# The recurrent stage of an RWKV-7 block: masks, squares and scaling by ScalarE, blocks picked by rows of 32, and one decay of the state

## The chip, the cores and the metric

The kernel runs on one core of a Trainium2 chip. The core has TensorE (PE), VectorE (DVE), ScalarE (ACT), GpSimd (POOL) and SyncE (SP), which here issues all transfers. The time is in device microseconds for the whole program, three transformer-like blocks over 2048 positions of width 1024. It is compared as the median over executions.

## The reference

The part that matters is the recurrence of the second block. It has 8 heads of 64 channels, and a 64 by 64 state per head that is decayed and changed at every position:

```python
def step(state, inp):
    rt, wt, kt, vt, kkt, at = inp
    sa = jnp.einsum('bhvk,bhk->bhv', state, -kkt)
    state = (state * wt[:, :, None, :]
             + sa[..., :, None] * (kkt * at)[..., None, :]
             + vt[..., :, None] * kt[..., None, :])
    yt = jnp.einsum('bhvk,bhk->bhv', state, rt)
    return state, yt

mean = jnp.mean(y, axis=-1, keepdims=True)
var = jnp.mean(jnp.square(y - mean), axis=-1, keepdims=True)
y = ((y - mean) * lax.rsqrt(var + GN_EPS)).reshape(B, S, D_RWKV)
y = y * gn_g.astype(jnp.float32) + gn_b.astype(jnp.float32)
bonus = jnp.sum((r_h * k_h * r_k).astype(jnp.float32), axis=-1, keepdims=True) * v_h.astype(jnp.float32)
y = y + bonus.reshape(B, S, D_RWKV)
```

The result is then multiplied by the silu of a gate. All of it is float32.

## The kernel before

The program is a row of stages, each with its own tiles (a prefix such as `rw_`) and semaphores. Every stage walks over 16 tiles of 128 positions. `rwkv` is the stage of the recurrence; an earlier one (`rwkv_project`) has stored r, kk, b, k, v and the gate, already multiplied by the decays inside a tile, in `packed`, and the decays across a tile in `totals` (`e_tot`, two factors per tile: to its middle, and from its middle to its end).

Within a tile the recurrence is a triangular system of 128 unknowns per head. Step i of the pipeline prepares tile i and, on the same engines, finishes tile t = i - 1. Each engine runs its own list in the order in which it is written, and waits on counting semaphores:

- TensorE multiplies b by kk and r (`multiply(i, pi, 0, r)`, L1569), which gives the products BA in banks 0 to 3, and later k by kk and r (banks 6, 7, 4, 5), which gives KA. In between it forms Z (`solve`, L1623 and L1626), four matmuls whose result nobody reads (the fillers, L1666), the rows of the 16 by 16 diagonal blocks spread over all partitions (`spread`, L1577 and L1578), the solution SA = XT Z, the output Y and the change of the state (`read_out`, L1636 to L1650).
- VectorE masks the products for the diagonal blocks and adds them up to a compact form (`compact_blocks`), masks BA, inverts all blocks of 16 together in 15 steps of two instructions (`invert_blocks`; tiles `outer` and `Ys`), writes the inverse into XT, renews the state S, and masks KA.
- The inverse then grows from blocks of 16 to 32, 64 and 128 in three levels (l = 4, 5, 6). At each, TensorE multiplies X by the corner of BA that joins two blocks (stage 0, L1600), ScalarE copies the product to T1 (L1730), TensorE multiplies by the inverse (stage 1, L1610 for X and L1613 for XT), and VectorE subtracts the result from X and XT. The corner is CT, which GpSimd makes as BA times a mask (L1748), two instructions of four heads per level.
- After levels 4 and 5, TensorE turns the inputs of tile i + 1 (`turn_two`, L1555) and ScalarE copies them (L1703 krT, L1705 bT and kT).
- The group norm of tile t runs on VectorE between the levels (`finish`: the mean, y less the mean, the squares and their sum), GpSimd takes the power -0.5, and in the next step `put_out` multiplies by gain and rstd and adds `rest`. GpSimd makes gain and rest (L1754 to L1766).

The state S is decayed twice in a tile, each time as a 128 by 512 product on VectorE (L1788): at the start of a step to the middle of the tile, and in `renew_state` to its end. Level 4's stage 1 waits for `inc_taken`, since it writes the bank from which the state's change is read. In the loop over tiles two steps stand in one iteration; the first three and the last two steps are written out.

## Time and profile before

| | |
|---|---|
| median of 3 runs | 4566.32 us (4563.86 to 4570.67) |
| the profiled execution | 4565.9 us, span 4563.8 us |
| mean granted TensorE clock | 0.963 |
| TensorE busy in the whole span | 4174.7 us (91%) |
| VectorE, ScalarE, GpSimd busy in the span | 2632.5, 1344.7, 633.4 us |
| the recurrent stage, first to last instruction | about 1702 to 2354 us |

The timeline lists an engine's instructions in order, with equal neighbours merged. "Idle before" in square brackets names what the profile holds for the releaser. Starts and durations of matmuls overlap, since they are pipelined, so the distance between two starts is the measure of pace. A group of 16 matmul records stands for 8 float32 matmuls.

### The profile page before, as it was taken

To read this page: it belongs to the slowest core of one execution; us is meant where nothing else is said; L and a number is where in the kernel's file an instruction comes from. 1 tells how busy PE (TensorE), PEld (TensorE's weight loads), DVE (VectorE), ACT (ScalarE), POOL (GpSimd) and SP (SyncE) were. 2 spreads that over 40 slices of the span, in tenths; PEclk is the share of its full clock that TensorE was granted. 3 is DMA by queue.
4 is the path that set the end of the run, shared out by engine and by line. 5 is a ranking of instruction groups with operands and counts; after the bars stand their busy time and mean duration, and the time that the engine had idled before them with its cause. 6 is when DMAs were issued, how large, how long until landed. Compare 5 with 4: busy or idle time off the path is not lost. (4 is left out here: it accounts for less than half of the span.)

```text
span 4563.8 us, 68323 instructions
## 1 busy us (share of the span) xinstructions
PE 4174.7 (91%) x24935; PEld 3522.7 (77%) x24992; DVE 2632.5 (58%) x5109; ACT 1344.7 (29%) x2721; POOL 633.4 (14%) x585
## 2 busy tenths in 40 slices
PE   9999799999799978999979996999989899899889
PEld 7888678887577758899978885778778677677667
DVE  5444444444566766888863345788743443677743
ACT  4323322222322221222221114666621211323221
POOL 0000011122000002333321110000000111122200
PEclk9999899999899988999989997999999999999989
DMA  3111311111444431111132325210034323423333
GB/s 147 49 64 64 130 62 63 62 62 55 168 135 140 140 123 53 50 48 48 49 115 110 115 101 172 77 35 20 10 139 164 129 103 135 135 90 98 99 132 115
DMA packets 218707, 434.13 MB, mean 95 GB/s; under 512 B 36819, under 2 KB 90836, under 8 KB 218422
## 3 DMA queue, kind: packets, MB, share of 16 engines
q1 hardware_dynamic: 218550, 432.09, 27.7%
q8 instruction: 93, 1.52, 0.1%
q14 instruction: 64, 0.52, 0.0%
HBM read 248.40 MB, written 146.93 MB: 87 GB/s over the span
## 5 line engine op out<-in xcount | busy, mean ns | idle before, releaser
L265 PE MATMUL rp_pj<-rp_w_high,rp_hT_high 128*128 128x512 f32 (+1 forms) x640 | 236.3, 378 | 22.7 <-DVE rp_gate L1429 17.8
L2569 DVE TENSOR_SCALAR_CACHE_REDUCE fa_sm<-fa_sc 128x512 f32<-128x512 f32 (+2 forms) x320 | 194.5, 610 | 92.6 <-PE fa_sc L2410 81.9
L265 PE MATMUL fp_pj<-fp_w_high,fp_hT_high 128*128 128x512 f32 (+2 forms) x640 | 216.5, 353 | 22.3 <-DMA fp_hT_low<-kept_low_dram 18.9
L266 PE MATMUL rp_pj<-rp_w_low,rp_hT_high 128*128 128x512 f32 (+1 forms) x640 | 231.5, 371 | 0.0
L266 PE MATMUL fp_pj<-fp_ahead_w_low,fp_hT_high 128*128 128x512 f32 (+2 forms) x640 | 214.5, 349 | 0.0
L265 PE MATMUL hg_pj<-hg_w_high,hg_hT_high 128*128 128x512 f32 x512 | 208.0, 406 | 4.6 <-DVE hg_w_low L255 4.6
L2424 PE MATMUL fa_tp<-fa_ident,fa_sm 128*128 128x128 f32 x1088 | 176.1, 283 | 33.1 <-DVE fa_pT_low L201 15.7
L2517 ACT CAST fa_pT_high<-fa_tp 128x512 fp32r<-128x512 f32 (+1 forms) x288 | 161.1, 560 | 148.5 <-PE fa_tp L2424 146.2
L265 PE MATMUL rc_pj<-rc_w_high,rc_hT_high 128*128 128x512 f32 (+1 forms) x512 | 190.1, 379 | 15.7 <-DMA rc_ident<-const_ident 10.1
L266 PE MATMUL hg_pj<-hg_w_low,hg_hT_high 128*128 128x512 f32 x512 | 201.5, 393 | 0.0
L201 DVE TENSOR_TENSOR fa_pT_low<-fa_tp,fa_pT_high 128x512 fp32r<-128x512 f32 (+1 forms) x288 | 189.0, 657 | 15.0 <-ACT fa_pT_high L2517 15.0
L2424 PEld LDWEIGHTS fa_tp<-fa_ident,fa_sm 128*128 128x128 f32 x1088 | 125.2, 142 | 93.8 <-DVE fa_pT_low L201 39.6
L2490 ACT ACTIVATE fa_sm<-fa_sm,fa_negtop 128x1024 f32<-128x1024 f32 (+4 forms) x192 | 173.7, 905 | 23.1 <-DVE fa_spare L2572 22.0
L2439 PE MATMUL fa_ov<-fa_pT_high,fa_values 128*128 128x256 f32 (+1 forms) x584 | 177.2, 325 | 0.0
L265 PEld LDWEIGHTS rp_pj<-rp_w_high,rp_hT_high 128*128 128x128 f32 x640 | 122.0, 191 | 59.1 <-ACT rp_hT_high L176 20.9
L265 PE MATMUL sw_pj<-sw_w_high,sw_hT_high 128*128 128x256 f32 (+1 forms) x512 | 151.5, 324 | 17.1 <-DMA sw_ident<-const_ident 13.6
L2409 PE MATMUL fa_sc<-fa_keysT,fa_qT_high 128*128 128x512 f32 (+2 forms) x320 | 164.0, 513 | 0.0
L265 PE MATMUL sh_pj<-sh_w_high,sh_hT_high 128*128 128x512 f32 x384 | 155.0, 404 | 6.7 <-ACT sh_hT_high L176 3.7
L2440 PE MATMUL fa_ov<-fa_pT_low,fa_values 128*128 128x256 f32 (+1 forms) x584 | 155.7, 284 | 0.0
L1748 POOL TENSOR_TENSOR rw_CT<-rw_BA,rw_blocks 128x512 f32<-128x512 f32 x96 | 127.3, 1347 | 174.6 <-DVE rw_BA L1788 96.1
L265 PEld LDWEIGHTS fp_pj<-fp_w_high,fp_hT_high 128*128 128x128 f32 x640 | 122.0, 191 | 38.0 <-DMA fp_hT_low<-kept_low_dram 19.1
L266 PE MATMUL sh_pj<-sh_ahead_w_low,sh_hT_high 128*128 128x512 f32 x384 | 151.3, 394 | 0.0
(571 smaller groups left out, 11185.0 us busy)
## 6 DMA issues: line engine op xcount, KB each, us to landing
rw_given<-rw_packed_dram SPq DMA_DIRECT2D x48, 512.0 KB, 3.9
rc_back<-rc_XB SPq DMA_DIRECT2D x48, 336.0 KB
rw_packed_dram<-rp_M SPq DMA_DIRECT2D x48, 256.0 KB, 2.6
rp_M<-rp_U SPq DMA_DIRECT2D x16, 728.0 KB, 4.7
hg_xt<-in_x SPq DMA_DIRECT2D x16, 512.0 KB, 3.7
kept_x_high_dram<-hg_hT_high SPq DMA_DIRECT2D x16, 512.0 KB, 3.5
kept_x_low_dram<-hg_hT_low SPq DMA_DIRECT2D x16, 512.0 KB, 4.3
sw_hT_high<-kept_x_high_dram SPq DMA_DIRECT2D x16, 512.0 KB, 3.7
```

The costliest lines, as they stand in the source:

```text
L201: return dve.tensor_tensor(part(self.low), whole, part(self.high).bitcast(F32), ALU.subtract)
L265: pe.matmul(out, hT.high[:, kc, :], high[:, kc, lo:hi], start=kc == 0, stop=False)
L266: pe.matmul(out, hT.high[:, kc, :], low[:, kc, lo:hi], start=False, stop=False)
L1748: pool.tensor_tensor(CT[:, 4 * g:4 * g + 4, :], BA[pi][:, 4 * g:4 * g + 4, 0, :], again(blocks[:, l - FIRST, :], 4), ALU.mult).then_inc(CT ...
L2409: pe.matmul(bank, qT[p].high[:, h, :], keysT[:, h, keys], start=False, stop=False)
L2424: one = pe.transpose(tp[at % 2][:, to:to + P], sm[:, block_at:block_at + P], ident[:])
L2439: pe.matmul(out[:, dst], values[:, 2 * k + m, h, :], parts.high[:, src], start=start, stop=False)
L2440: return pe.matmul(out[:, dst], values[:, 2 * k + m, h, :], parts.low[:, src], start=False, stop=stop)
L2490: act.activation(view, view, ACT.Exp, bias=negtop[:, unit(n, p) % 16:unit(n, p) % 16 + 1], accum_out=total[j % 2][p][:, i, h:h + 1]).then_ ...
L2517: act.copy(pT[at % 3].high[:, 0:cols], tp[at % 2][:, 0:cols]).then_inc(p_high, 1)
L2569: dve.tensor_scalar(sm[:, to:to + cols], bank_of(slot)[:, 0:cols], 0.0, NEG, ALU.add, ALU.max, accum_out=tops[:, four, c:c + 1]).then_inc( ...
```

## The change

ScalarE takes over three things. `corners` copies the corner blocks of BA into two CT tiles, one for level 4 and one for level 5, that GpSimd has cleared once at the start: six copies per tile, between its copies Z and SA. `square` forms (y - mean) squared per head with an accumulator, four heads after level 4's copies and four after level 5's, and `scale_y` applies rstd and -mean*rstd per head before the next Z copy. GpSimd's six corner products go; it gains a small product (`shift`), and its gain and rest are put behind `parts_ready` and `S_in`. VectorE loses the difference, the squares, their sum and the product with rstd. At the top level no corner is needed: stage 0 takes rows 0 to 63 of BA itself, and stage 1 rows 64 to 127 of T1 and XT.

`compact_blocks` reads all four product banks in one instruction for each 32 partitions, only the 32 columns that belong to them, and adds the two halves of 16. S is decayed once: by the product of this tile's second factor and the next tile's first, in `renew_state`. `inc_taken` is raised at its first instruction. `put_out` moves from before level 4 to level 5. The transfer of b and k (`load_bk`) no longer waits for `rest_ready`, and the change of the state is not formed for the last tile. One constant (`blocks`, 192 KB) is no longer loaded. The fillers stay as they are.

```diff
@@ tensor @@
                 if stage == 0:
-                    pe.wait_ge(CT_ready, done + g + 1)
+                    if not top:
+                        pe.wait_ge(CT_ready, 2 * i + l - FIRST + 1)
                     pe.wait_ge(X_ready, done + g + 1)
-                    width = P // 2 if top else P
                     for h in hs:
-                        last = pe.matmul(B[2 * g][:, (h % 4) * P:(h % 4) * P + width], CT[:, h, :], X[:, h, 0:width], start=True, stop=True)
+                        at = (h % 4) * P
+                        if top:
+                            last = pe.matmul(B[2 * g][:, at:at + HALF], BA[pi][0:HALF, h, 0, :], X[0:HALF, h, 0:HALF], start=True, stop=True)
+                        else:
+                            last = pe.matmul(B[2 * g][:, at:at + P], CT[l - FIRST][:, h, :], X[:, h, :], start=True, stop=True)
...
-                        lhs, rows_ = (T1[:, h, 0:HALF], HALF) if top else (T1[:, h, :], P)
-                        last = pe.matmul(B[2 * g + 1][0:rows_, 4 * HALF + (h % 4) * HALF:4 * HALF + (h % 4 + 1) * HALF], lhs, halves_of(XT[pi][:, h, :], l, 1), start=True, stop=True)
+                        lower = slice(HALF, P) if top else slice(0, P)
+                        last = pe.matmul(B[2 * g + 1][:, 4 * HALF + (h % 4) * HALF:4 * HALF + (h % 4 + 1) * HALF], T1[lower, h, :], halves_of(XT[pi][lower, h, :], l, 1), start=True, stop=True)
@@ scalar @@
+            def corners(i, pi):
+
+                act.wait_ge(masked, 8 * i + 4)
+                for l in range(FIRST, LEVELS - 1):
+                    w = 1 << l
+                    for at in range(0, P, 2 * w):
+                        one = act.copy(CT[l - FIRST][at:at + w, :, at + w:at + 2 * w], BA[pi][at:at + w, :, 0, at + w:at + 2 * w])
+                    one.then_inc(CT_ready, 1)
+
+            def square(t, pt, some):
+                act.wait_ge(neg_ready, t + 1)
+                for h in some:
+                    cols = slice(h * RW_DIM, (h + 1) * RW_DIM)
+                    one = act.activation(spare[:, cols], y[pt][:, cols], ACT.Square, bias=negmean[:, h:h + 1], accum_out=squares[:, h:h + 1])
+                one.then_inc(squared, 1)
+
+            def scale_y(u, pu):
+
+                act.wait_ge(rstd_ready, u + 1)
+                for h in range(RW_HEADS):
+                    cols = slice(h * RW_DIM, (h + 1) * RW_DIM)
+                    one = act.activation(y[pu][:, cols], y[pu][:, cols], ACT.Identity, bias=shift[:, h:h + 1], scale=rstd[:, h:h + 1])
+                one.then_inc(y_scaled, 1)
@@ vector @@
-                for r in range(2):
-                    dve.wait_ge(products, 4 * i + r + 1)
-                    for o in range(2):
-                        tt(X[:, 4 * r + o:4 * r + 4:2, :], heads(B[PRODUCT_BANKS[0][r][o]][:], 2)[:, :, 0:P], again(near[:], 2), ALU.mult)
-                dve.drain()
-                dve.tensor_reduce(Uc[:], X[:].rearrange("p h (b t) -> p h t b", t=SMALL), AX, ALU.add)
+                dve.wait_ge(products, 4 * i + 2)
+                for q in range(0, P, 2 * SMALL):
+                    own = slice(q, q + 2 * SMALL)
+                    tt(own32[own], low_banks[own, :].rearrange("p (s c) -> p s c", s=RW_HEADS)[:, :, own], again(near[own, own], RW_HEADS), ALU.mult)
+                dve.drain()
+                by_bank = own32[:].rearrange("p (r o k) c -> p o r k c", r=2, o=2)
+                by_head = Uc[:].rearrange("p (r k o) t -> p o r k t", r=2, k=2)
+                for o in range(2):
+                    tt(by_head[:, o], by_bank[:, o, :, :, 0:SMALL], by_bank[:, o, :, :, SMALL:], ALU.add)
...
+                tt(renewal[:], e_tot[pt][:, :, 1], e_tot[pi][:, :, 0], ALU.mult)
                 dve.wait_ge(inc_done, t + 1)
-                tt(heads(inc[:], PAIRS), heads(B[INC_BANK][:], PAIRS), again(own_head[:], PAIRS), ALU.mult)
+                tt(heads(inc[:], PAIRS), heads(B[INC_BANK][:], PAIRS), again(own_head[:], PAIRS), ALU.mult).then_inc(inc_taken, 1)
                 dve.drain()
                 tt(S[:], S[:], heads(inc[:], PAIRS), ALU.add)
                 dve.drain()
-                decay(pt, 1).then_inc(inc_taken, 1)
...
+                tt(S[:], S[:], spread(renewal[:], P), ALU.mult).then_inc(S_in, 1)
```

On ScalarE, from level 4's X copies to the next Z copy of a steady step, the list was:

```order
L1725 COPY rw_X<-rw_b 128x512 x2
L1730 COPY rw_T<-rw_b 128x512 x2
L1703 COPY rw_krT<-rw_b 128x4x128 x2
L1730 COPY rw_T<-rw_b 128x512 x2
L1705 COPY rw_bT<-rw_b 128x512
L1705 COPY rw_kT<-rw_b 128x512
L1730 COPY rw_T<-rw_b 128x4x64 x2
L1715 ACTIVATE rw_Z<-rw_b 128x512
```

In the changed kernel the same place reads as follows (`spare` is a tile that nobody reads):

```order
L1764 COPY rw_X<-rw_b 128x512 x2
L1771 COPY rw_T<-rw_b 128x512 x2
L1713 COPY rw_krT<-rw_b 128x4x128 x2
L1730 ACTIVATE rw_spare,rw_squares<-rw_y,rw_negmean 128x64 x4
L1771 COPY rw_T<-rw_b 128x512 x2
L1715 COPY rw_bT<-rw_b 128x512
L1715 COPY rw_kT<-rw_b 128x512
L1730 ACTIVATE rw_spare,rw_squares<-rw_y,rw_negmean 128x64 x4
L1769 COPY rw_T<-rw_b 64x4x64 x2
L1738 ACTIVATE rw_y<-rw_y,rw_shift,rw_rstd 128x64 x8
L1751 ACTIVATE rw_Z<-rw_b 128x512
```

The squares stand between the copies of the turned inputs and the T1 copies of the next level, and the scaling before Z.

On VectorE, from the state to the end of level 5 of a step that has a tile before and no output to put yet, the list was:

```order
L1788 TENSOR_TENSOR rw_S<-rw_S,rw_e_tot 128x512
L1788 TENSOR_TENSOR rw_KA<-rw_b,rw_causal 128x2x256 x4
L1788 TENSOR_TENSOR rw_X<-rw_X,rw_b 128x16x16
L1788 TENSOR_TENSOR rw_XT<-rw_XT,rw_b 128x16x16
L1788 TENSOR_TENSOR rw_X<-rw_X,rw_b 128x16x16
L1788 TENSOR_TENSOR rw_XT<-rw_XT,rw_b 128x16x16
L1847 TENSOR_REDUCE rw_mean<-rw_y 128x8
L1849 TENSOR_SCALAR rw_mean<-rw_mean 128x8
L1788 TENSOR_TENSOR rw_y<-rw_y,rw_mean 128x512
L1788 TENSOR_TENSOR rw_X<-rw_X,rw_b 128x8x32
```

Now it is:

```order
L1826 TENSOR_TENSOR rw_S<-rw_S,rw_renewal 128x512
L1826 TENSOR_TENSOR rw_KA<-rw_b,rw_causal 128x2x256 x4
L1887 TENSOR_REDUCE rw_negmean<-rw_y 128x8
L1890 TENSOR_SCALAR rw_negmean<-rw_negmean 128x8
L1826 TENSOR_TENSOR rw_X<-rw_X,rw_b 128x16x16
L1826 TENSOR_TENSOR rw_XT<-rw_XT,rw_b 128x16x16
L1826 TENSOR_TENSOR rw_X<-rw_X,rw_b 128x16x16
L1826 TENSOR_TENSOR rw_XT<-rw_XT,rw_b 128x16x16
L1826 TENSOR_TENSOR rw_X<-rw_X,rw_b 128x8x32
```

The mean has moved ahead of level 4's subtraction, and the difference y - mean is gone.

## Rows read from the trace of the kernel before

**Rows 1.** Windows: length; busy PE, PEld, DVE, ACT, POOL (instructions); PE clock; DMA.
```profile
1992.64:2030.92 38.28, 36.70 (x317) 34.27 (x317) 32.33 (x72) 8.09 (x15) 15.11 (x11) 1.00 0.15 48
2030.92:2068.78 37.86, 36.40 (x317) 34.34 (x317) 32.27 (x70) 8.09 (x16) 15.06 (x11) 1.00 0.15 49
```

**Rows 2.** Timeline, TensorE: start, duration, engine, line, operation, tiles; the fillers.
```profile
1992.41 1.18 PE L1666 MATMUL rw_b<-rw_pick_row 128*128 128x512 f32 x4
```

**Rows 3.** Timeline, TensorE, the levels of one tile to the next tile's products.
```profile
2046.76 2.02 PE L1600 MATMUL rw_b<-rw_X,rw_CT 128*128 128x128 f32 x16 [0.33 <-ACT rw_X L1725]
2049.01 1.08 PE L1610 MATMUL rw_b<-rw_T,rw_XT 128*128 128x64 f32 x8 [0.22 <-DVE rw_S L1788]
...
2052.60 1.04 PE L1555 MATMUL rw_b<-rw_ident,rw_given 128*128 128x128 f32 x8
2054.05 2.02 PE L1600 MATMUL rw_b<-rw_X,rw_CT 128*128 128x128 f32 x16 [0.40 <-DVE rw_X L1788]
2055.91 1.05 PE L1610 MATMUL rw_b<-rw_T,rw_XT 128*128 128x64 f32 x8
...
2059.47 1.04 PE L1555 MATMUL rw_b<-rw_ident,rw_given 128*128 128x128 f32 x8
2060.36 1.90 PE L1600 MATMUL rw_b<-rw_X,rw_CT 128*128 128x64 f32 x16
2062.18 1.21 PE L1613 MATMUL rw_b<-rw_XT,rw_T 128*64 128x64 f32 x16
2063.89 2.00 PE L1569 MATMUL rw_b<-rw_krT,rw_bT 64*128 64x256 f32 x16 [0.50 <-DVE rw_XT L1788]
```

**Rows 4.** Timeline, VectorE: first row step, second decay, level 4's update, compaction.
```profile
2034.48 1.09 DVE L1788 TENSOR_TENSOR rw_Ys<-rw_Ys,rw_outer 128x120 f32<-128x120 f32 x1
...
2047.26 1.60 DVE L1788 TENSOR_TENSOR rw_S<-rw_S,rw_e_tot 128x512 f32<-128x512 f32 x1
...
2053.49 0.41 DVE L1788 TENSOR_TENSOR rw_X<-rw_X,rw_b 128x256 f32<-128x256 f32 x1
...
2067.12 1.89 DVE L1809 TENSOR_REDUCE rw_Uc<-rw_X 128x128 f32<-128x1024 f32 x1
```

**Rows 5.** Timeline, ScalarE in an earlier stage, activations with an accumulator.
```profile
1000.35 0.49 ACT L923 ACTIVATE sw_sm<-sw_sm,sw_negtop 128x256 f32<-128x256 f32 x1
1000.75 0.19 ACT L923 ACTIVATION_READ_ACCUMULATOR sw_sm<-sw_sm,sw_negtop 128x1 f32 x1
1000.84 0.49 ACT L923 ACTIVATE sw_sm<-sw_sm,sw_negtop 128x256 f32<-128x256 f32 x1
```

**Rows 6.** Timeline, ScalarE: SA, then the copies around levels 5 and 6.
```profile
2039.89 0.59 ACT L1717 COPY rw_SA<-rw_b 128x512 f32<-128x512 f32 x1 [8.37 <-PE rw_b L1636]
...
2053.24 1.07 ACT L1703 COPY rw_krT<-rw_b 128x512 f32<-128x512 f32 x2 [3.84 <-PE rw_b L1555]
...
2060.60 0.59 ACT L1705 COPY rw_kT<-rw_b 128x512 f32<-128x512 f32 x1
2061.39 0.37 ACT L1730 COPY rw_T<-rw_b 128x256 f32<-128x256 f32 x1 [0.20 <-PE rw_b L1600]
```

**Rows 7.** Groups by form, weight loads of the stage: busy, mean ns, idle before.
```profile
L1569 PEld LDWEIGHTS rw_b<-rw_krT,rw_bT 64*128 64x128 f32 x256 | 24.1, 186 | 12.4 <-DVE rw_XT L1788 7.7 <-issue 3.1
```

**Rows 8.** TensorE in steps 15 and 16, and the window behind the first.
```profile
2320.44 3.55 PE L1600 MATMUL rw_b<-rw_X,rw_CT 128*128 128x128 f32 x16 [1.29 <-DVE rw_X L1788]
2331.83 0.38 PE L1623 MATMUL rw_b<-rw_S,rw_krT 128*128 128x128 f32 x1 [1.29 <-DVE rw_S L1788]
2322.00:2323.50 1.50, 1.50 (x9) 1.50 (x8) 1.35 (x3) 0.59 (x1) 1.13 (x1) 0.50 0.05 11
```

**Rows 9.** Timeline, the last tile's y copy, its power and its output.
```profile
2341.90 0.59 ACT L1721 COPY rw_y<-rw_b 128x512 f32<-128x512 f32 x1 [2.09 <-PE rw_b L1646]
2350.86 2.01 POOL L1773 TENSOR_TENSOR rw_rstd<-rw_var,rw_power 128x8 f32<-128x8 f32 x1 [13.88 <-DVE rw_var L1859]
2353.67 0.69 DVE L1788 TENSOR_TENSOR rw_out<-rw_y,rw_rest 128x512 f32<-128x512 f32 x1
```

More of the change, by code:

```diff
@@ L1452, in rwkv @@
         given_of = lambda p, n: given[p][:, AT[n]:AT[n] + RW]
-        mean, var, rstd = (sb(n, [P, RW_HEADS]) for n in ("mean", "var", "rstd"))
+        negmean, squares, var, rstd, shift = (sb(n, [P, RW_HEADS]) for n in ("negmean", "squares", "var", "rstd", "shift"))
+        renewal = sb("renewal", [P, PAIRS])
         krT = [sb(f"krT{p}", [P, PAIRS, 2, P]) for p in range(2)]
@@ L1647, in read_out @@
                 last.then_inc(y_done, 1)
-                for p in range(PAIRS):
-                    cols = slice(p * P, (p + 1) * P)
-                    last = pe.matmul(B[INC_BANK][:, cols], given_of(pt, "b")[:, cols], SA[:, cols], start=False, stop=p == PAIRS - 1)
-                last.then_inc(inc_done, 1)
+                if i is not None:
+                    for p in range(PAIRS):
+                        cols = slice(p * P, (p + 1) * P)
+                        last = pe.matmul(B[INC_BANK][:, cols], given_of(pt, "b")[:, cols], SA[:, cols], start=False, stop=p == PAIRS - 1)
+                    last.then_inc(inc_done, 1)
             def step(i, hi, pi, t, ht, pt):
@@ L1738, in _ @@
             pool.memset(power[:], -0.5)
+            for one in CT:
+                pool.memset(one[:], 0.0)
             pool.drain()
@@ L1788, in tt @@
                 return dve.tensor_tensor(out_, a_, b_, op)
-            def decay(p, half):
-                return tt(S[:], S[:], spread(e_tot[p][:, :, half], P), ALU.mult)
             def mask_products(i, pi, n, r):
@@ L1905, in step @@
                         dve.drain()
+                    if m:
+                        variance(t)
                 elif m:
-                    for part in range(2):
-                        finish(t, ht, pt, part)
+                    put_out(t - 1, 1 - pt)
+                    mean(t, ht, pt)
+                    variance(t)
                     put_out(t, pt)
```

122 lines of the change are left out of this document (58 added, 64 removed).

## The prediction, made before the changed kernel was run

> **What bounds the kernel now.** Only one of the kernel's stages changes, the recurrent one (tiles `rw_`), so the profile's shares over the whole span say little. I read first the windows cut at every `Z` copy, which give the length of one row tile: 38.28 and 37.86 us in turn, with TensorE (PE) busy for 36.7 and 36.4 of them, VectorE (DVE) for 32.3, ScalarE (ACT) for 8.1, GpSimd (POOL) for 15.1, at granted clock 1.00 [rows 1]. So TensorE is the bound, with about 1.5 us of idle time in a tile, and whatever leaves VectorE or GpSimd pays only where TensorE waits for it. Then I followed TensorE through a tile by the timeline.
>
> First half (from the products of tile i to the transposes of the first inverse, about 19.3 us): TensorE has no idle row in it. Even where `spread` waits for VectorE's compacted blocks there stand the four filler matmuls, 1.18 us long [rows 2].
>
> Second half (the three levels): the idle spells are here. Level 4's corrections start at 2049.01, 2.25 us behind its T1 products, while at level 5 the same step comes 1.86 us behind (2054.05 to 2055.91) [rows 3]: VectorE's second decay of S, 1.60 us long and begun at 2047.26, ends at 2048.86 [rows 4], and `inc_taken` hangs on it. Level 5's products start at 2054.05, not 0.89 us behind the transposes of 2052.60 as at level 6 (2059.47 to 2060.36), which would be 2053.49 [rows 3]: 0.56 us for the update of X, which VectorE starts only at 2053.49, behind `put_out` [rows 4]. The last wait is the 0.50 us before the next tile's products, for the last update of XT [rows 3].
>
> **What VectorE and GpSimd lose, and why most of it is off the path.** Compaction: four masks over 256 elements stay four masks over 256 elements (on 32 partitions each), and the reduction of 1.89 us [rows 4] becomes two additions of 64 elements, some 0.4 us with their drain. But the masks now wait for both products, 1 us later than the first of them today. Net the blocks are ready 0.5 to 0.8 us earlier. In the steady tiles TensorE can't use that: it is then still in `solve` and in the fillers. Only tiles whose blocks come late gain; these are the 38.28 us ones, so their 0.42 us go, **-0.21 us** per tile in the mean [rows 1]. GpSimd's six corner products go, and with them VectorE's stalls beside them: `Ys` at the first row step takes 1.09 us [rows 4] where the next one takes about 0.28. The inverse is thus finished 1.5 us earlier, but the transposes that take it come when TensorE gets there, so nothing more is gained. One decay instead of two, and `inc_taken` at its first step, do pay: the 2.25 us of level 4 fall to 1.86, **-0.39 us** [rows 3]. At level 5 VectorE will be ready before 2053.49 - 0.4, since S, its stalls and `put_out` (which moves to level 5) leave the stretch before; that would be -0.56 us, were it not for the squares.
>
> **What ScalarE gains.** Corner copies (six of 128 or 256 elements) lie between the Z and SA copies, where ScalarE idles 8.37 us [rows 6]. The y scaling (eight instructions) lies before the Z copy, whose result is wanted by the matmuls that this idle time ends with. Both at nothing; with a copy of 256 elements at 0.37 us and the squares' price below as upper ends they come to 2.2 and 2.7 us, together under the 8.37, and would cost that if the cover were gone.
>
> The squares are different: they are four instructions with an accumulator each, placed between the copies of the turned inputs and the T1 copies of the next level, for which TensorE waits in order. Price of one: of the pairs ACTIVATE plus accumulator read over 256 elements one starts every 0.49 us [rows 5]; less 192 elements at (0.59 - 0.37)/256 us = 0.84 ns [rows 6] is 0.33 us, so four take 1.32 us. By the Trainium skill, "ScalarE: Activation LUTs", section "What ACT_TABLE_LOAD costs", an ACTIVATE with a pointer bias takes 280 ns + 0.833 ns per element and overlaps the next by 93 ns, 0.24 us here without a price for the accumulator read; four would be 0.96 us by it, and each path term below 0.36 us less. The 0.49 us row includes the read and decides.
>
> Level 5: the two krT copies start at 2053.24 and take 1.07 us; the next can start at 2054.20 [rows 6]. Squares to 2055.52, T1 copy 0.59 to 2056.11, and 0.15 us to the waiting matmul (X ends at 2053.90, TensorE starts at 2054.05 [rows 3, 4]): 2056.26 instead of 2055.91, **+0.35 us**, the 0.56 us gain included.
>
> Level 6: kT copy starts at 2060.60, the next can start at 2061.08 [rows 6]; squares to 2062.40, copy 0.37 to 2062.77, plus 0.15 is 2062.92 instead of 2062.18 [rows 3]: **+0.74 us**.
>
> **The top level's matmuls.** Both stages now contract over 64 rows. Stage 0 keeps its 128 weight columns: nothing. Stage 1 takes all 128 columns of T1 where it took 64. Eight such matmuls with 64 weight columns take 1.21 us, eight with 128 columns 1.90 us [rows 3]; their end is what VectorE's last XT update waits for, so **+0.69 us**. Half as many weight rows don't help: a weight load over 64 rows and 128 columns takes 186 ns in the mean [rows 7], and the eight products of 64 rows at 2063.89 take 2.00 us, no less than those of 128 rows [rows 3]. The Trainium skill ("TensorE: Matmul & The Clock Gate", section "LDWEIGHTS (loading the stationary operand)") has the same rule, columns and not contraction rows, at columns/1.2 ns: sixteen loads would be 0.85 us more by it; it speaks against this edit. The bounds of the term are 0 (if 64 rows did halve the load) and 0.85.
>
> **Sum.** Per steady tile -0.21 - 0.39 + 0.35 + 0.74 + 0.69 = +1.18 us; there are 14 with squares on the path (steps 1 to 14): +16.5.
> First tile (no squares; here VectorE bounds the first half): -0.7 for the compaction, -0.8 for the stall, +0.69: -0.8. The 192 KB constant that is not loaded: taken as nothing, at best 1 us.
> Step 15 has no transposes of a next tile, so squares are ready before T1. TensorE waited 1.29 us for X behind `put_out`, the granted clock went to 0.50, and the products took 3.55 us where 2.02 is usual [rows 3, 8]. VectorE will be in time, so -1.29 - 1.53 - 0.39 + 0.69 = -2.5.
> Last step: the wait of 1.29 us for S before `solve` [rows 8] goes. Behind the y copy (2342.49) to the end of out (2354.36) stand 11.87 us [rows 9]; now it is 0.9 for the mean, 2.8 for eight squares, 0.2 for the variance, 2.0 for the power [rows 9] and 0.2 to 1.3 for the shift, 2.8 for the scaling (at the squares' price), 1.5 for two products, and five handings over of 0.1 to 0.15: 10.9 to 12.3. I take 11.4, near the short end, since eight elements are few: -0.5. Together -1.8.
> Total +16.5 - 0.8 - 2.5 - 1.8 = **+11.4 us**. The profiled execution took 4565.9 us (span 4563.8), within 0.5 us of the median 4566.3, so the forecast is **4577 us**, +0.24%. Waits that a loop must compute for the new instructions are not in it.
>
> **Rivals.**
> *A. The two added costs are smaller.* If a pair of square and read costs 0.2 us (an accumulator read alone is 0.19 [rows 5]), level 5 comes to -0.18 and level 6 to +0.21: 14 x 1.06 = 14.8 us less, 4562. If the top level's wide weights cost nothing, 16 x 0.69 = 11 us less, 4566; both, 4551. For it: no row has 64 elements with an accumulator. Against: both prices come from rows of the same kind.
> *B. Faster: the squares never meet T1.* Their place is the point: four must fit into the 0.45 us between 2054.20 and the T1 copy, wanted half of stage 0 and a handing over (some 1.15 us) behind 2053.49, and the 0.59 us between 2061.08 and 2061.67, so it decides at 0.11 to 0.15 us each. Then level 5 gives -0.53 and level 6 nothing: -0.44 per tile, 14 x = -6.2, with the ends (-5.1) -11.3: 4554.6; with the wide weights at nothing 4544. Against it stands the 0.49 us pace [rows 5].
> *C. The clock falls.* A wait of 1.29 us led to clock 0.50 and 1.53 us lost, while another of 1.29 us (2331.83) did not [rows 8]. The new waits are about 0.75 us at level 5, and 0.65 at level 6 with the 0.50 behind it. Should it fall once in every steady tile, 14 x 1.5 = +21: 4598. The Trainium skill ("TensorE: Matmul & The Clock Gate", "Part 1: The HAM clock gate") has the rule that an idle TensorE is set back from 2.4 to 1.2 GHz; the trace agrees with the fall, and leaves open whether these shorter waits do it.
> *D. In the steady tiles nothing changes,* as the matmuls stay and the delays just fill today's waits: then only the ends count, -5.1 us, about 4561.
>
> **How the numbers follow.** Forecast 46% (its own range 4570 to 4585), A and D together 26%, B 14%, C 14%. The range takes in the cheap bounds of A down to B's nearer value and most of C: 4554 to 4596. What a measurement can tell from no change is about 0.2%, 9 us: below 4557 is faster, above 4575.5 slower. Faster is B's 14% and 2% of A; slower is C's 14% and two thirds of the forecast's; the rest is same: 0.16, 0.40, 0.44.
>
> **What would show it.** Tile length near 39.2 us and no longer alternating; the T1 copy of level 5 starting 1.3 us after the last krT copy could let it go, with four pairs of ACTIVATE and read at 0.33 us between; TensorE idle about 0.75 us before the level 5 corrections and 0.65 before those of level 6; the top stage 1 at 1.9 us; no wait for S and none for X at level 5; clock 1.00 throughout, step 15 included. GpSimd busy falls by about 127 us and VectorE's by some 100, with nothing to show for it. Wrong would make it: T1 copies without delay (squares cheap), a top stage of 1.2 us, or tiles whose matmuls take double time.

## The result, and the profile after

The changed kernel took **4618.41 us** (median of 4 runs, 4614.71 to 4632.21), the kernel before 4568.49 us in the same session (4563.86 to 4572.66): a ratio of 1.0114, with an interval of 1.0102 to 1.0127. The forecast was 4577 us with a range up to 4596. Slower was right; 41 us of it were not foreseen. The profiled execution took 4632.21 us (span 4630.2) and is the slowest of the four.

First the windows cut at every `Z` copy, to be held against [rows 1] (columns: window, length, busy time of PE, PEld, DVE, ACT and POOL with the number of instructions, granted clock, DMA):

```profile
1849.19:1896.54 47.35, 45.74 (x317) 42.87 (x317) 26.22 (x73) 15.46 (x46) 8.98 (x8) 0.79 0.14 40
1896.54:1950.79 54.25, 52.12 (x317) 48.41 (x317) 21.73 (x65) 15.14 (x45) 4.61 (x5) 0.71 0.11 35
1950.79:1991.78 40.99, 38.86 (x317) 36.17 (x317) 23.69 (x68) 15.26 (x45) 6.68 (x7) 0.96 0.15 45
1991.78:2032.78 41.00, 38.87 (x317) 36.18 (x317) 23.70 (x68) 15.25 (x45) 6.66 (x7) 0.96 0.15 45
```

Nine of the fourteen steady tiles look like the last two rows: 41.0 us, at clock 0.96, where the kernel before had 38.28 and 37.86 at 1.00. VectorE and GpSimd lost what the change takes off them (32.3 to 23.7 us and 15.1 to 6.7 us in a tile), ScalarE rose from 8.1 to 15.3.

TensorE in the last of these windows, from level 5 to the next tile's products, the places of [rows 3] (start, duration, engine, line, operation, tiles; in brackets the idle time before it and what ended it):

```profile
2013.87 1.95 PE L1609 MATMUL rw_b<-rw_X,rw_CT 128*128 128x128 f32 x16
2016.68 1.10 PE L1619 MATMUL rw_b<-rw_T,rw_XT 128*128 128x64 f32 x8 [0.87 <-ACT rw_T L1771]
...
2021.28 2.00 PE L1607 MATMUL rw_b<-rw_X,rw_BA 64*128 64x64 f32 x16
2023.79 2.00 PE L1622 MATMUL rw_b<-rw_XT,rw_T 64*128 64x64 f32 x16 [0.52 <-ACT rw_T L1769]
2026.29 3.41 PE L1576 MATMUL rw_b<-rw_krT,rw_bT 64*128 64x256 f32 x16 [0.50 <-DVE rw_XT L1826]
```

The first four rows are the ones forecast: idle 0.87 us at level 5 (forecast about 0.75) and 0.52 at level 6 (0.65), and a top stage 1 of 2.00 us (1.9). The fifth is not. The same eight products (sixteen records) took 2.00 us before [rows 3]; now they take 3.41. Windows of one microsecond show the granted clock over them:

```profile
2025.00:2026.00 1.00, 0.79 (x8) 0.65 (x6) 0.52 (x2) 0.00 (x0) 0.00 (x0) 1.00 0.00 0
2026.00:2027.00 1.00, 0.71 (x6) 0.61 (x8) 0.41 (x2) 0.00 (x0) 0.34 (x1) 0.86 0.00 0
2027.00:2028.00 1.00, 1.00 (x8) 0.84 (x6) 0.00 (x0) 0.00 (x0) 1.00 (x1) 0.50 0.00 0
...
2029.00:2030.00 1.00, 1.00 (x5) 0.37 (x2) 0.26 (x1) 1.00 (x4) 0.00 (x0) 0.50 0.00 0
2030.00:2031.00 1.00, 1.00 (x10) 1.00 (x10) 0.97 (x3) 1.00 (x4) 0.00 (x0) 0.93 0.00 0
```

The clock falls from 2.4 to 1.2 GHz some 0.4 us after the products have begun, and is back only just past 2030, with TensorE busy throughout. It does so in one tile after another. Fifteen groups of these products stand behind a top level; these are the first, the second and the fourteenth:

```profile
1759.49 2.00 PE L1576 MATMUL rw_b<-rw_krT,rw_bT 64*128 64x256 f32 x16 [0.59 <-DVE rw_XT L1826]
1799.24 3.78 PE L1576 MATMUL rw_b<-rw_krT,rw_bT 64*128 64x256 f32 x16 [0.60 <-DVE rw_XT L1826]
...
2313.37 3.68 PE L1576 MATMUL rw_b<-rw_krT,rw_bT 64*128 64x256 f32 x16 [0.51 <-DVE rw_XT L1826]
```

Fourteen of the fifteen take 3.3 to 3.8 us; the one of 2.00 stands behind the first tile, the only one without squares. In ten of the fourteen the fall begins in the products, in three shortly before, in the top level's stage 1. In the tile of 1849 to 1896 it begins earlier still, inside level 5, with all 128 rows in use, about 2 us after the end of the new wait:

```profile
1874.09 1.10 PE L1619 MATMUL rw_b<-rw_T,rw_XT 128*128 128x64 f32 x8 [0.87 <-ACT rw_T L1771]
1875.03 1.06 PE L1622 MATMUL rw_b<-rw_XT,rw_T 128*128 128x64 f32 x8
1875.92 1.34 PE L1619 MATMUL rw_b<-rw_T,rw_XT 128*128 128x64 f32 x8
1877.06 1.91 PE L1622 MATMUL rw_b<-rw_XT,rw_T 128*128 128x64 f32 x8
```

There the half clock does not go back before the next tile but lasts on, through these windows:

```profile
1876.00:1900.00 24.00, 23.50 (x111) 21.42 (x110) 7.74 (x21) 8.46 (x27) 4.13 (x4) 0.51 0.03 13
1900.00:1924.00 24.00, 24.00 (x112) 22.75 (x111) 11.24 (x37) 1.17 (x2) 1.14 (x1) 0.50 0.05 18
```

**Where the 66.4 us between the two profiled spans (4563.8 and 4630.2) are.** From the first to the fifteenth `Z` copy it was 2297.22 - 1764.12 = 533.10 us before and is 2363.85 - 1764.35 = 599.50 now: 66.4 us, all of it. (At the ends 4.3 us are won, and 1.6 and 2.8 us lost ahead of the stage and behind it, where the code is the same.) A tile without the fall would be 41.00 less 1.41 us for the products and 0.23 for the `solve` behind them (2.93 us from 2029.63 to the fillers of 2032.56; 2.70 at full clock in the trace of `top_full`), 39.36 us, which the forecast put at 39.2. Fourteen such tiles are 17.9 us more than before; the sum had 16.5. The other 599.5 - 14 x 39.36 = **48.5 us are the clock**. Nine tiles lose 1.6 us each and two (42.43 and 42.41 us long) 3.1 each, together 21; in these every fall begins at the top level or right behind it. The rest, 27.5 us, lies in three windows (47.35, 54.25 and, from 2319.91, 43.94 us): one holds the start and one the end of the long spell, the third a second fall inside level 5 (its row at 2347.53 takes 1.86 us instead of 1.06) besides the one at the top level.

### The profile page after: what moved, and what is told of

The parts are those of the page before. It is cut to its first block and busy times, and to the rows that moved or that the text cites. A ratio compares the mean times of both kernels' runs of the same rounds, so it can differ in the third digit from the quotient of the medians.

```text
span 4630.2 us, 68530 instructions
## 1 busy us (share of the span) xinstructions
PE 4234.0 (91%) x24976; PEld 3572.8 (77%) x24976; DVE 2495.3 (54%) x5057; ACT 1460.2 (32%) x3201; POOL 501.6 (11%) x507
## 3 DMA queue, kind: packets, MB, share of 16 engines
q8 instruction: 93, 1.52, 0.1%
## 5 line engine op out<-in xcount | busy, mean ns | idle before, releaser
L269 PE MATMUL rp_pj<-rp_w_high,rp_hT_low 128*128 128x512 f32 (+1 forms) x640 | 144.3, 368 | 0.0
```

Of the source, the lines that this page charges most:

```text
L269: last = pe.matmul(out, hT.low[:, kc, :], high[:, kc, lo:hi], start=False, stop=kc == KC - 1)
```

## The experiments

After the result there were two theories on what makes the clock fall. **W**: the new idle time of TensorE in front of the T1 copies, as in rival C. **K**: the top level's matmuls, which after the change contract over 64 rows in both stages and stand directly ahead of `multiply`, whose 64 rows were always there [rows 7]. None of the kernels leaves out a part of the computation. The table is the overview; "tile" is the length of an undisturbed steady tile (clock 1.00), and "slow" is how many of the fifteen groups of `multiply`'s first products that stand behind a top level take over 2.9 us instead of 2.00 in the profiled execution, which is what the fall looks like. The count is that of one execution, and the median can be that of others: the profiled one took 4574.49 us in `squares_late` and 4570.48 in `top_full`, well under the medians, and 4622.52 in `before_top64`, well over.

| kernel | median us (runs) | ratio, interval | tile us | slow |
|---|---|---|---|---|
| before | 4568.49 (4) | 1 | 38.28, 37.86 | 0 of 15 |
| after | 4618.41 (4) | 1.0114, 1.0102 to 1.0127 | none | 14 of 15 |
| squares_late | 4595.37 (7) | 1.0053, 1.0038 to 1.0068 | 37.33 | 6 of 15 |
| narrow_top | 4622.21 (4) | 1.0123, 1.0106 to 1.0140 | 39.45 | 13 of 15 |
| wait_fillers | 4614.40 (4) | 1.0102, 1.0085 to 1.0119 | none | 15 of 15 |
| before_dummies | 4578.70 (10) | 1.0019, 1.0010 to 1.0029 | 38.83, 38.70 | 0 of 15 |
| top_full | 4579.24 (7) | 1.0021, 1.0009 to 1.0032 | 38.23 | 0 of 15 |
| late_full | 4548.89 (5) | 0.9956, 0.9943 to 0.9970 | 36.71 | 0 of 15 |
| before_top64 | 4610.32 (4) | 1.0085, 1.0070 to 1.0100 | 38.44 | 12 of 15 |
| late_stage0_64 | 4556.02 (7) | 0.9970, 0.9959 to 0.9981 | 36.91 | 2 of 15 |
| late_stage1_64 | 4564.58 (10) | 0.9993, 0.9984 to 1.0002 | 37.50 | 0 of 15 |
| late_rows | 4544.89 (5) | 0.9952, 0.9938 to 0.9965 | 36.71 | 0 of 15 |
| late_spaced | 4575.85 (10) | 1.0016, 1.0006 to 1.0026 | 37.41 | 5 of 15 |

### First round: squares away, columns back, waits filled, squares alone

**squares_late**: the changed kernel with its eight squares behind the top level's T1 copies.

```diff
-                        if m and l < FIRST + 2:
-                            square(t, pt, range(4 * (l - FIRST), 4 * (l - FIRST) + 4))
+                    if m:
+                        for n in range(2):
+                            square(t, pt, range(4 * n, 4 * n + 4))
```

> The changed kernel with all eight squares behind the top level's T1 copies instead of four after level 4's and four after level 5's copies; nothing is left out. Theory W (the squares make TensorE wait 0.87 us at level 5 and 0.52 us at level 6, and this idle time makes the granted clock fall once per tile): both waits go, the clock is 1.00 in all steady tiles, and a tile takes 37.9 us less 0.39 and 0.56 plus 0.69 for the wide top matmuls, 37.4 to 37.7 us; the kernel takes 4553 to 4560 us. Rival K (the clock falls because of the top level's 64-row matmuls): one fall per tile stays, tiles of 39 to 39.5 us, 4580 to 4590 us.

**narrow_top**: of each four matmuls of the top stage 1, three take 64 columns of T1 again; the rows stay at 64.

```diff
+                        wide = HALF if top and h % 4 else P
-                        last = pe.matmul(B[2 * g + 1][:, 4 * HALF + (h % 4) * HALF:4 * HALF + (h % 4 + 1) * HALF], T1[lower, h, :], halves_of(XT[pi][lower, h, :], l, 1), start=True, stop=True)
+                        last = pe.matmul(B[2 * g + 1][0:wide, 4 * HALF + (h % 4) * HALF:4 * HALF + (h % 4 + 1) * HALF], T1[lower, h, 0:wide], halves_of(XT[pi][lower, h, :], l, 1), start=True, stop=True)
```

> The changed kernel with three of every four stage-1 matmuls of the top level back at 64 weight columns; squares stay where they are. Nothing is left out. Theory W: the two T1 waits of 0.87 and 0.52 us stay, so one fall of the clock per tile stays; the path is 0.4 to 0.5 us shorter per tile, 7 us in all, 4605 to 4615 us. Rival K: the clock stays at 1.00 and the time comes to 4568 to 4575 us.

**wait_fillers**: between the two stages of level 5 two, and of level 6 one matmul of 128 rows by 512 columns, whose result nobody reads.

```diff
+                        for n in range({FIRST + 1: 2, LEVELS - 1: 1}.get(l, 0) if m and follows else 0):
+                            pe.matmul(B[6 if l == FIRST + 1 else 4][:], pick_row[:, n, :], pick_row[:, 4:8, :].rearrange("p n t -> p (n t)"), start=True, stop=True)
```

> The changed kernel with two matmuls whose result nobody reads in TensorE's wait before level 5's stage 1 and one in that before level 6's (512 columns each), in the steps that have a next tile. The path is the same, only the idle time is filled. Theory W: the clock stays at 1.00, tiles take 39.2 to 39.5 us, the kernel 4574 to 4582 us, which is also what the path alone costs. If idle time is not what makes the clock fall: 4610 to 4620 us as the changed kernel, or more if the fillers delay the path.

**before_dummies**: the kernel before with eight squares of a constant, with accumulators that nobody reads, at the places of the change.

```diff
+                        if m and l < FIRST + 2:
+                            need(act, dummied, 2 * t + l - FIRST)
+                            for h in range(4):
+                                one = act.activation(spare_[:, h * RW_DIM:(h + 1) * RW_DIM], causal2[:, 0, (h % 2) * RW_DIM:(h % 2 + 1) * RW_DIM], ACT.Square, bias=power[:, h:h + 1], accum_out=sums_[:, h:h + 1])
+                            one.then_inc(dummied, 1)
```

> The kernel before with the squares' load alone: four ACTIVATE with accumulator of 64 columns (on a constant, results unused) after level 4's krT copies and four after level 5's kT copy. Theory W: TensorE waits for T1 0.35 us longer at level 5 (before the X update is late too) and 0.74 us at level 6, tile 38.9 to 39.3 us at full clock, 4580 to 4584 us, and if the clock falls as in the changed kernel one fall per tile of 1.5 to 1.7 us more, 4602 to 4620 us. Rival K: no fall, 4580 to 4584 us. Squares without effect on TensorE: 4566 us.

Measured. The list of TensorE's waits from 1840 to 2270 (what waited, for whom: us in total, times, longest) in `wait_fillers`:

```profile
PE rw_b L1576 <- DVE rw_XT L1828: 5.6, 11, 0.5
PE rw_b L1619 <- ACT rw_T L1773: 4.0, 10, 0.4
```

and in `before_dummies`:

```profile
PE rw_b L1614 <- ACT rw_T L1732: 6.3, 11, 0.6
PE rw_b L1570 <- DVE rw_XT L1795: 5.6, 11, 0.5
```

`wait_fillers` halves the wait for T1 at level 5 (0.9 to 0.4 us) and has none left at level 6, and the clock falls in 15 tiles of 15. `before_dummies` puts 0.6 us of new idle time into every tile, at level 6, beside the 0.5 and 0.4 us that were there, and the clock falls in none; the wait of 0.87 us at level 5 it does not bring, and its median of 4578.70 us is 1.3 under the range expected. `squares_late` has no wait for T1 at all and still falls in 6 of 15 tiles; K had expected it in all. Its profiled execution took 4574.49 us; five of the seven took 4594 to 4601, above K's range, with a mean granted clock of 0.951 to 0.953 where the profiled one has 0.958. So **W is out for the falls at the products**: they stay when the waits are filled, and come when there are none. The case of all the waits without the 64 rows is `top_full`, in the next round. `narrow_top` missed both ranges: K had counted on its clock coming back, and it doesn't (4622 us), although a tile that escapes the fall takes 39.45 us. What is narrower there is the columns; the 64 rows are as in the change. `before_dummies` also gives the squares a price on the path of the old kernel without any change of clock: 38.77 - 38.07 = 0.70 us per tile.

### Second round: the top level's rows, taken away and put in alone

**top_full**: the changed kernel with its top level as before: a third matrix with corner and zeros, copied by ScalarE, both stages over 128 rows, 64 columns of T1; squares where the change has them.

```diff
-        CT = [sb(f"CT{l}", [P, RW_HEADS, P]) for l in range(FIRST, LEVELS - 1)]
+        CT = [sb(f"CT{l}", [P, RW_HEADS, P]) for l in range(FIRST, LEVELS)]
...
-                            last = pe.matmul(B[2 * g][:, at:at + HALF], BA[pi][0:HALF, h, 0, :], X[0:HALF, h, 0:HALF], start=True, stop=True)
+                            last = pe.matmul(B[2 * g][:, at:at + HALF], CT[l - FIRST][:, h, :], X[:, h, 0:HALF], start=True, stop=True)
...
-                        lower = slice(HALF, P) if top else slice(0, P)
+                        wide = HALF if top else P
-                        last = pe.matmul(B[2 * g + 1][:, 4 * HALF + (h % 4) * HALF:4 * HALF + (h % 4 + 1) * HALF], T1[lower, h, :], halves_of(XT[pi][lower, h, :], l, 1), start=True, stop=True)
+                        last = pe.matmul(B[2 * g + 1][0:wide, 4 * HALF + (h % 4) * HALF:4 * HALF + (h % 4 + 1) * HALF], T1[:, h, 0:wide], halves_of(XT[pi][:, h, :], l, 1), start=True, stop=True)
```

> The changed kernel with its top level as before the change: both stages of level 6 contract over all 128 rows again (a third matrix with the corner of 64 x 64 and zeros beside it, copied by ScalarE), and stage 1 takes 64 columns of T1. Nothing else is undone; the squares stay ahead of the T1 copies. Theory K (the matmuls of 64 rows at the top level make the clock fall right behind them): the granted clock stays at 1.00 through the steady tiles, a tile is 41.0 less 1.7 for the fall less 0.7 for the 64 columns, 38.6 us, and the kernel comes back to 4560 to 4575. Theory P (the path is longer and the pieces of work of each tile are further apart, whatever the top level): the clock goes on falling once in most tiles, a tile is 40.3, the time 4600 to 4612.

**late_full**: the same, and the squares behind the top level as in `squares_late`.

> The same undo of the top level, and all eight squares behind the top level's T1 copies. Theory K: clock 1.00, tiles of 37.3 less 0.7 for the 64 columns plus at most 0.4 where TensorE now meets another wait, 36.6 to 37.0 us, the time 4543 to 4556, faster than the kernel before. Theory P: tiles of 37 to 38.5 with falls of the clock in about three of five, as with the squares moved alone, 4570 to 4590.

**before_top64**: the kernel before with the change's top level on TensorE and nothing else of the change.

```diff
-                        last = pe.matmul(B[2 * g][:, (h % 4) * P:(h % 4) * P + width], CT[:, h, :], X[:, h, 0:width], start=True, stop=True)
+                        if top:
+                            last = pe.matmul(B[2 * g][:, (h % 4) * P:(h % 4) * P + HALF], BA[pi][0:HALF, h, 0, :], X[0:HALF, h, 0:HALF], start=True, stop=True)
...
-                        lhs, rows_ = (T1[:, h, 0:HALF], HALF) if top else (T1[:, h, :], P)
+                        lower = slice(HALF, P) if top else slice(0, P)
+                        last = pe.matmul(B[2 * g + 1][:, 4 * HALF + (h % 4) * HALF:4 * HALF + (h % 4 + 1) * HALF], T1[lower, h, :], halves_of(XT[pi][lower, h, :], l, 1), start=True, stop=True)
```

> The kernel before with only TensorE's top level changed as in the change (stage 0 over rows 0 to 63 of BA and X, stage 1 over rows 64 to 127 of T1 and XT, with all 128 columns of T1); masks, squares, decays and T1 copies as before. Theory K: the granted clock falls right behind the top level in most tiles, at least 1.5 us each, so 4566 + 15 x (0.7 + 1.7) = 4600 or more. Theory P: the clock stays at 1.00 and only the 128 columns cost, 15 x 0.69 = 10 us, 4577.

Measured. `top_full`, TensorE from level 5 on, the same places as in the trace of after above:

```profile
2020.23 1.10 PE L1618 MATMUL rw_b<-rw_T,rw_XT 128*128 128x64 f32 x8 [0.73 <-ACT rw_T L1770]
...
2024.73 1.90 PE L1606 MATMUL rw_b<-rw_X,rw_CT 128*128 128x64 f32 x16
2027.20 1.15 PE L1621 MATMUL rw_b<-rw_XT,rw_T 128*64 128x64 f32 x16 [0.57 <-ACT rw_T L1768]
2028.85 2.00 PE L1576 MATMUL rw_b<-rw_krT,rw_bT 64*128 64x256 f32 x16 [0.50 <-DVE rw_XT L1825]
```

The waits are those of the changed kernel (0.73, 0.57 and 0.50 us idle, where it has 0.87, 0.52 and 0.50), and the products take 2.00 us, in this tile and in all fifteen. One fall is left in the steady tiles of this trace, at a cost of 1.6 us, inside level 5 behind the wait of 0.73 us:

```profile
2214.15 1.89 PE L1621 MATMUL rw_b<-rw_XT,rw_T 128*128 128x64 f32 x8
```

Falls that begin inside level 5 stand in three traces, two in the changed kernel, three in `narrow_top` and this one, and all three kernels have the wait of 0.87 or 0.73 us before it. None of the ten other traces has such a wait, nor a fall at that place in a steady tile. For these falls W fits, then; no run tested it by itself. Now `before_top64`, in which no wait of the change exists:

```profile
1995.39 1.77 PE L1601 MATMUL rw_b<-rw_X,rw_BA 64*128 64x64 f32 x14
...
1997.23 1.72 PE L1616 MATMUL rw_b<-rw_XT,rw_T 64*128 64x64 f32 x14
1999.46 3.64 PE L1569 MATMUL rw_b<-rw_krT,rw_bT 64*128 64x256 f32 x16 [0.50 <-DVE rw_XT L1791]
```

and a window with a long spell in the same kernel:

```profile
2206.46:2248.35 41.89, 41.06 (x317) 38.42 (x317) 33.75 (x74) 8.08 (x15) 15.18 (x12) 0.88 0.13 44
2248.35:2301.95 53.60, 52.77 (x317) 49.25 (x317) 29.37 (x68) 8.08 (x15) 14.74 (x11) 0.68 0.11 34
```

The top level over 64 rows is **enough** to make the clock fall in 12 tiles of 15 of the old kernel, long spell included, at a price of 43 us, of which the columns are some 10; and taking it out of the changed kernel ends the falls at this place in the execution that was traced. Both are within what K expected, but for 4 us of the median of `top_full`: its runs go from 4563.85 to 4585.17, the profiled one is among the short ones (4570.48, mean clock 0.962), and the four that took 4579 to 4585 us have a mean clock of 0.957 to 0.959, so they lose by the clock, at a place that no trace shows. `late_full` came in as K said, 4548.89 us, and beats the kernel before.

### Third round: which stage, rows alone, and a gap

Here the changed kernel's own operands serve for 128 rows: `BA` and `X` whole, since the other half of `X` holds zeros in the columns used, and T1 whole, since the upper half of `XT` does. **late_rows** differs from `squares_late` in these lines and no others:

```diff
-                            last = pe.matmul(B[2 * g][:, at:at + HALF], BA[pi][0:HALF, h, 0, :], X[0:HALF, h, 0:HALF], start=True, stop=True)
+                            last = pe.matmul(B[2 * g][:, at:at + HALF], BA[pi][:, h, 0, :], X[:, h, 0:HALF], start=True, stop=True)
...
-                        lower = slice(HALF, P) if top else slice(0, P)
-                        last = pe.matmul(B[2 * g + 1][:, 4 * HALF + (h % 4) * HALF:4 * HALF + (h % 4 + 1) * HALF], T1[lower, h, :], halves_of(XT[pi][lower, h, :], l, 1), start=True, stop=True)
+                        wide = HALF if top else P
+                        last = pe.matmul(B[2 * g + 1][0:wide, 4 * HALF + (h % 4) * HALF:4 * HALF + (h % 4 + 1) * HALF], T1[:, h, 0:wide], halves_of(XT[pi][:, h, :], l, 1), start=True, stop=True)
...
-                                act.copy(T1[HALF:P, 4 * g:4 * g + 4, 0:HALF], heads(B[2 * g][HALF:P, :], 4)[:, :, 0:HALF]).then_inc(T1_ready, 1)
+                                act.copy(T1[:, 4 * g:4 * g + 4, 0:HALF], heads(B[2 * g][:], 4)[:, :, 0:HALF]).then_inc(T1_ready, 1)
```

> Squares behind the top level's T1 copies, both stages of the top level over 128 rows with the change's own operands (BA and X whole, whose other half multiplies zeros), 64 columns of T1, and no third matrix. It differs from the kernel with the squares moved in nothing but rows and columns of the top level's sixteen matmuls and the rows of two T1 copies. Theory K: clock 1.00, tiles of 36.7 us, 4544 to 4553, as with the third matrix, so that it is the rows and not the matrix or its copy. If the third matrix had done it by its timing: falls come back, above 4570.

**late_stage0_64** leaves stage 0 as in the change and has the second and third piece of that diff; **late_stage1_64** has its first piece alone.

> Squares behind the top level's T1 copies, and of the top level only stage 0 contracts over 64 rows (as in the change); stage 1 goes over 128 rows with 64 columns of T1. Theory K in its simple form (eight matmuls of 64 rows are as good as any other eight): falls become rarer than with both stages (three in five tiles of 37.3 to 39.1), tiles mostly 36.7, 4552 to 4562. If stage 1, which stands directly before `multiply`, is what does it: clock 1.00 in all tiles, 4546 to 4552. If stage 0 alone does it: as with both stages, tiles less 0.7, 4580 to 4588.

> Squares behind the top level's T1 copies, and of the top level only stage 1 contracts over 64 rows, with 128 columns of T1 (as in the change); stage 0 goes over all 128 rows of BA and X. Without any fall tiles would be 37.3 and the time 4548.9 + 14 x 0.6 = 4557. If stage 1 does it: falls in about three of five tiles, 4580 to 4595. If it takes both: none or few, 4555 to 4563.

**late_spaced** is `squares_late` with two unread matmuls between the top level and the next tile's products.

```diff
+                    for n in range(2 if m and follows else 0):
+                        pe.matmul(B[4][:], pick_row[:, n, :], pick_row[:, 4:8, :].rearrange("p n t -> p (n t)"), start=True, stop=True)
```

> Squares behind the top level's T1 copies, the top level over 64 rows as in the change, and two matmuls of 128 rows by 512 columns whose result nobody reads between the top level and the products of the next tile, that is in the wait of 0.50 us for XT. The question is whether the clock falls because the sixteen matmuls of the top level stand directly before sixteen more of 64 rows (`multiply`), with only idle time between. If that stretch has to be unbroken: no falls, tiles of 37.3 + 0.1 us, 4555 to 4563. If a short piece of full work and the filled wait change nothing: falls in about three of five tiles as without the fillers, 4575 to 4600.

Measured. A steady tile of `late_rows`, and the end of one on TensorE:

```profile
1982.49:2019.20 36.71, 35.97 (x319) 34.30 (x317) 23.76 (x68) 15.47 (x46) 6.75 (x7) 1.00 0.16 50
```

```profile
2009.13 1.90 PE L1607 MATMUL rw_b<-rw_X,rw_BA 128*128 128x64 f32 x16
2010.96 1.21 PE L1622 MATMUL rw_b<-rw_XT,rw_T 128*64 128x64 f32 x16
2012.67 2.00 PE L1576 MATMUL rw_b<-rw_krT,rw_bT 64*128 64x256 f32 x16 [0.50 <-DVE rw_XT L1827]
```

Clock 1.00 in all tiles and 4544.89 us, against 4595.37 with 64 rows. In the profiled executions, both short, the difference is 34 us: 21 from the first to the fifteenth `Z` copy, 3 ahead of the first and 9 behind the last, where the half clock holds from 2330 to 2371 in `squares_late` and from 2313 to 2333 in `late_rows`. With 128 columns and 64 rows in stage 1 alone (`late_stage1_64` against `late_rows`) a tile is 37.50 instead of 36.71 us and its clock 1.00, so the 128 columns by themselves do not bring the fall. **Neither stage does it often alone**: stage 1 over 64 rows gives 0 slow groups of 15 (its time is 1.6 us over what was expected of it), stage 0 gives 2 of 15 (and so nearly the first of its three expectations), both 6 of 15, and 14 of 15 with the squares at the change's place. It looks like a dose of such matmuls, and not like one instruction. `late_spaced` has, in place of the wait of 0.50 us, this:

```profile
2025.56 1.72 PE L1622 MATMUL rw_b<-rw_XT,rw_T 64*128 64x64 f32 x14
2027.21 0.73 PE L1702 MATMUL rw_b<-rw_pick_row 128*128 128x512 f32 x2
2027.88 2.00 PE L1576 MATMUL rw_b<-rw_krT,rw_bT 64*128 64x256 f32 x16
```

It still falls in 5 tiles of 15. TensorE is busy for 37.18 us of a free tile's 37.42, and the one wait left in the list is of 0.2 us, at level 4, so these falls need no idle time near them. The second expectation fits by its time, at the lower end, with fewer falls than it had: a filled wait and full work between the two groups do not cure it. The median of `late_spaced` lies 20 us below that of `squares_late`, but two of that kernel's seven runs are as short (4574.49 and 4574.93), and the two traces are alike (5 and 6 of 15), so it isn't shown that they help the time.

The slow groups are not scattered. In the changed kernel the row grows by about 0.04 us from tile to tile (3.33, 3.37, 3.41 us and so on to 3.68), so the fall comes a little earlier in the work each time; in `squares_late` they come in pairs, with two or three free tiles between. The moment at which the 64-row matmuls come, and not only their number, may thus decide how often the clock falls. A change of the squares' place or of one stage also changes the tile's length, and no run sets the two apart.

## Why the prediction was wrong, by its own steps

**Bound now.** Right: TensorE bounds the stage, and what left VectorE and GpSimd (8.6 and 8.4 us per tile) shows nowhere but in the waits that the prediction names. The list of TensorE's waits in the changed kernel, from 1753 to 2400, has none for S and none for X from VectorE any more:

```profile
PE rw_b L1619 <- ACT rw_T L1771: 12.1, 14, 0.9
PE rw_b L1576 <- DVE rw_XT L1826: 7.8, 15, 0.6
PE rw_b L1622 <- ACT rw_T L1769: 6.7, 13, 0.5
PE rw_b L1609 <- ACT rw_X L1764: 3.9, 15, 0.3
```

**The gains (-0.21, -0.39, and the 0.56 us inside level 5).** Right, somewhat low: together 1.16 us by the sum; `late_rows`, where nothing added stands against them, has 36.71 us against a mean of 38.07 before, 1.36.

**The squares (+0.91 at level 5 before that gain, +0.74 at level 6).** Right. The pace was worked out at 0.33 us from rows of 256 elements, and it is that:

```profile
2014.73 0.35 ACT L1730 ACTIVATE rw_spare<-rw_y,rw_negmean 128x64 f32<-128x64 f32 x1
2014.98 0.19 ACT L1730 ACTIVATION_READ_ACCUMULATOR rw_spare<-rw_y,rw_negmean 128x1 f32 x1
2015.08 0.33 ACT L1730 ACTIVATE rw_spare<-rw_y,rw_negmean 128x64 f32<-128x64 f32 x1
...
2015.41 0.33 ACT L1730 ACTIVATE rw_spare<-rw_y,rw_negmean 128x64 f32<-128x64 f32 x1
```

From one ACTIVATE to the next it is 0.35 and 0.33 us, so the row that held the accumulator read was the one to go by. The estimate by the rule of the Trainium skill ("ScalarE: Activation LUTs", section "What ACT_TABLE_LOAD costs"), 0.24 us without the read, is too low here. Forecast together 1.65 us per tile; `top_full` less `late_full` is 38.23 - 36.71 = 1.52. Rival A's half on the squares falls with this, and so do B and D.

**The top level's columns (+0.69).** Right as a term: 37.33 - 36.71 = 0.62 with both stages over 64 rows (`squares_late` against `late_rows`), 0.79 with stage 1 alone, and 0.85 from the top stage 1 to the products where a wait stands before it (2.50 us from 2023.79 to 2026.29, 1.65 us in `top_full`). Half the rows save no time: "Half as many weight rows don't help" holds, with stage 0 alone over 64 rows a tile is even 0.20 us longer (36.91).

**The step that failed** is the one behind it: this part weighed 64 rows against 128 only by the time of a weight load and a matmul at full clock. That the rows also count for the clock was neither in the sum nor in a rival, and the sign "clock 1.00 throughout" went with it. The clock term stood at nothing in the sum and was 48.5 us in the profiled execution; the 64 rows alone, in the kernel before, cost 43 us of its median, some 10 of them for the columns (`before_top64`). Rival C had the size right per fall ("once in every steady tile, 14 x 1.5 = +21"; measured 1.6) and most of the places wrong: it put the cause on the idle time of the new waits, and `wait_fillers`, `late_spaced` and `top_full` take that away for the falls at the top level and behind it. For the two falls inside level 5, and the long spell that one of them opened, C may be right. It also took every fall to be as short as the one of [rows 8]; the long spell has no counterpart there. With 14% for C, and its price as the upper end, the range could not reach 4618.

**The ends (-5.1).** Measured -4.3. The first tile (first transposes to first `Z` copy) went from 47.09 to 45.73 us, -1.4 (forecast -0.8). Step 15 (between the last two `Z` copies, which takes in the start of the last step) went from 37.54 to 35.93, -1.6, at clock 1.00 and with no wait for X or for S, as said; but its `Z` copy comes late:

```profile
2397.67 2.08 ACT L1738 ACTIVATE rw_y<-rw_y,rw_shift,rw_rstd 128x64 f32<-128x64 f32 x6
2399.78 0.60 ACT L1751 ACTIVATE rw_Z<-rw_b 128x512 f32<-128x512 f32 x1
...
2400.52 1.75 PE L1645 MATMUL rw_b<-rw_Z,rw_XT 128*128 128x64 f32 x14 [0.85 <-ACT rw_Z L1751]
```

The scaling of y was put at nothing because the work behind `Z` covers it; in the last step there is no `multiply` in front of `solve`, so the cover is gone and 0.85 us of it stand on the path. From the last `Z` copy to the end of the output it was 19.60 us and is 18.23, -1.4; both stretches together are -3.0, where the forecast had -2.5 - 1.8 = -4.3. Not in it either: the clock falls behind this wait, and the output's matmuls take 3.68 us (at 2403.32) where they took 1.90. The part behind the y copy came out better, at 10.4 us instead of 11.4: the squares' eight at 0.33 us as worked out, the power 1.64 us and not the 2.01 of [rows 9].

**The chances.** Slower had 44%, the forecast's mechanism and C's. What would have been due is a case of its own for the clock under each new form of matmul that the kernel had nowhere else in such number; [rows 7] and [rows 3] already showed the products of 64 rows that stand next to the new ones.

## What to carry to other kernels

A matmul over half the rows took no less time here than one over all, and enough of them in a row (the two stages of the top level, thirty-two records of the trace, ahead of sixteen of the same kind) brought the clock of a busy TensorE to 1.2 GHz in 5 to 15 tiles of 15, by the kernel. If the other half of the operands holds zeros anyway, contract over it: that one edit is worth 50 us of the median here (4595.37 to 4544.89), and 34 us between the two executions that were traced. Work that is moved to an idle engine has to be placed behind that engine's deliveries to the bound engine, not only into its idle time: the squares cost 1.5 us per tile at one place and nothing in a steady tile at another (the last step, where nothing covers them, is the exception: TensorE waits 2.24 us for `Z` in `late_rows` and 0.85 in the changed kernel), and with both put right the change gives 4544.89 us, 0.48% less than before (interval 0.35 to 0.62%).

## What the runs showed of the hardware that was not expected

The granted clock fell while TensorE was busy, with idle time of 0.5 us ahead of it that the kernel before has as well, and only with both stages of the top level over 64 rows often. The Trainium skill ("TensorE: Matmul & The Clock Gate", "Part 1: The HAM clock gate") ties the fall to an idle engine and the full clock to a busy one; the wait of 1.29 us and the fall behind it in the kernel before [rows 8] agree with that. The falls of `before_top64`, without a new wait, and of `late_spaced`, with hardly any wait left, do not, nor does the stretch from 1900 to 1924 in the changed kernel, in which TensorE is busy for 24.00 us of 24.00 at clock 0.50. So an engine that the trace counts as busy can still be granted the half clock.

What stays open: why the place of the squares changes how often it falls (14 of 15 against 6 of 15), although their wait at level 6 alone, in `before_dummies`, brings none and filling the waits, in `wait_fillers`, removes none; whether number or moment of the 64-row matmuls decides; whether the wait at level 5 brings the falls inside it; what ends a long spell; and where the longer runs of `top_full`, 4579 to 4585 us, lose their clock.
